# Two transformer blocks on one core: another order of splits, products and norm sums in nine stages, and x times the mixed rows' root in place of the reciprocal

## The reference

```python
# block one
h = rmsnorm(x, g_mix); z = h @ w_in                       # 1024 x 2560: b_gate, c_gate, x_in, u, v
y_conv = b_gate * conv3(c_gate * x_in)                    # 512 channels, 3 taps, causal
y_sgu  = gelu(u) * (tril(w_spatial) @ layernorm(gelu(v), g_sgu) + b_spatial)   # 8 heads, chunks of 128
x = x + concat(y_conv, y_sgu) @ w_out                     # 1024 x 1024
t = rmsnorm(x, g_ffn)
# router: top 1 of 4 groups, top 2 of its 8 experts; y = sum over 32 experts, each weighted per token
x = x + sum_e((silu(t @ w_gate[e]) * (t @ w_up[e]) * comb_e) @ w_down[e])       # d_expert 512
x = x + sigmoid(rmsnorm(x, g_ple) @ w_ple_gate) * (p @ w_ple_proj)              # p: 256 wide
x = rmsnorm(x, g_final)
# block two
h = rmsnorm(x, norm_mix_pre); proj = h @ w_in_2           # 1024 x 4608: conv_in, q, k, v, g_conv, g_att
u = silu(layernorm(conv31(glu(conv_in)), ...)); conv_out = u @ w_conv_branch + b
att_out = stick_breaking_attention(q, k, v) @ w_att_branch                      # 8 heads of 64
mix = (sigmoid(g_conv) * conv_out + sigmoid(g_att) * att_out) @ w_out_2
x = x + rmsnorm(mix, norm_mix_post)
gate, up = split(rmsnorm(x, norm_ffn_pre) @ w_ffn_up)     # 1024 x 5632
x = x + rmsnorm((silu(gate) * up) @ w_ffn_down, norm_ffn_post)                  # 2816 x 1024
```

## Time and profile before

| | |
|---|---|
| time before, median of 3 runs | 989.81 us (988.94 to 992.14) |
| the profiled execution's own time | 990.13 us |
| its span in the trace | 988.4 us |
| PE busy | 946.4 us (96%) |
| DVE busy | 497.4 us (50%) |
| ACT busy | 330.3 us (33%) |
| chain that ended last | PE 87%, DVE 7%, ACT 3%, issue 2%, DMA 1% |
| mean rate of the loads over the span | 293 GB/s |

### The profile page before, as it was taken

How to read it: one execution, slowest core, us unless ns; L and a number is a source line. 1 busy time by engine, 2 the same in 40 slices (tenths; PEclk the granted TensorE clock), 3 DMA queues, 4 the chain that set the end, 5 groups by cost and what they waited for, 6 DMA issues and landing times.

```text
span 988.4 us, 14242 instructions
## 1 busy us (share of the span) xinstructions
PE 946.4 (96%) x5926; PEld 670.2 (68%) x5926; DVE 497.4 (50%) x866; ACT 330.3 (33%) x527; POOL 36.1 (4%) x39
## 2 busy tenths in 40 slices
PE   6999999999999899999899899999999899999997
PEld 6997734444434444444344689978989899999885
DVE  6595612222222223222122776979898667676632
ACT  5823210101011010101001657555566555544531
POOL 1000000000000000000000000222310000000000
PEclk9999999999999999999999999999999999999999
DMA  8956999999999999999999942532433424555301
GB/s 324 406 233 260 424 407 427 420 430 432 429 430 431 426 431 430 431 430 431 431 425 419 432 189 115 212 129 96 161 133 124 170 107 180 189 201 200 128 1 42
DMA packets 28981, 289.45 MB, mean 293 GB/s; under 512 B 3056, under 2 KB 6384, under 8 KB 12400
## 3 DMA queue, kind: packets, MB, share of 16 engines
q1 hardware_dynamic: 28192, 286.91, 70.9%
q10 hardware_dynamic: 720, 1.57, 0.4%
HBM read 287.43 MB, written 1.05 MB: 292 GB/s over the span
## 4 chain that ended last, share of the span: by engine, by line
PE 87%; DVE 7%; ACT 3%; issue 2%; DMA 1%; SPq 0%; DVEq 0%; ACTq 0%
PE ps L282 86%; DVE wl L278 2%; DVE arena L1531 1%; ACT wh L271 1%; DMA arena<-in_xT 1%; PE ps L1045 1%; DVE arena L589 0%; ACT arena L1835 0%; DVE arena L1737 0%; ACT arena L1838 0%; DVE arena L378 0%; PE ps L2017 0%; ACT in_h L660 0%; DVE arena L1439 0%; DVE arena L584 0%
## 5 line engine op out<-in xcount | busy, mean ns | idle before, releaser
L282 PE MATMUL ps<-ring,arena 128*64 128x512 f32 x1216 | 340.1, 599 | 7.0 <-issue 6.7
L282 PEld LDWEIGHTS ps<-ring,arena 128*64 128x64 f32 x1216 | 109.7, 138 | 166.9 <-issue 164.6
L278 DVE TENSOR_TENSOR wl<-ring,wh 128x1024 fp32r<-128x1024 f32 x150 | 180.2, 1232 | 59.6 <-ACT wh L271 59.4
L271 ACT ACTIVATE wh<-ring 128x1024 fp32r<-128x1024 f32 x150 | 151.0, 1049 | 38.5 <-PE ps L282 28.2
L282 PE MATMUL ps<-arena 128*64 128x512 f32 (+3 forms) x416 | 161.4, 538 | 0.7 <-DVE arena L584 0.5
L1150 DVE SCALAR_TENSOR_TENSOR arena<-ps,arena 128x512 f32<-128x512 f32 x16 | 12.0, 750 | 205.7 <-PE ps L282 205.7
L282 PE MATMUL ps<-up_h,wh 128*128 128x256 f32 x352 | 87.0, 285 | 3.9 <-ACT up_h L1937 3.9
L282 PEld LDWEIGHTS ps<-arena 128*64 128x64 f32 (+1 forms) x416 | 53.2, 141 | 47.0 <-issue 41.2
L282 PE MATMUL ps<-up_l,wh 128*128 128x256 f32 x352 | 83.0, 283 | 0.0
L1220 ACT ACTIVATE y_h<-ps 128x512 fp32r<-128x512 f32 x32 | 19.1, 597 | 158.1 <-PE ps L282 158.1
L282 PEld LDWEIGHTS ps<-up_h,wh 128*128 128x128 f32 x352 | 67.1, 191 | 4.3 <-issue 4.3
(11 more groups left out here) (263 smaller groups left out, 1508.0 us busy)
## 6 DMA issues: line engine op xcount, KB each, us to landing
ring<-in_moe SPq DMA_DIRECT2D x69, 2048.0 KB, 24.2
arena<-in_moe SPq DMA_DIRECT2D x17, 2048.0 KB, 25.9
ring<-in_w_in SPq DMA_DIRECT2D x12, 2048.0 KB, 10.5
ring<-in_w_up SPq DMA_DIRECT2D x11, 2048.0 KB, 7.7
ring<-in_moe SPq DMA_DIRECT2D x20, 512.0 KB, 15.0
ring<-in_w_dn SPq DMA_DIRECT2D x5, 2048.0 KB, 7.7
ring<-in_w_out SPq DMA_DIRECT2D x4, 2048.0 KB, 15.9
arena<-in_moe SPq DMA_DIRECT2D x12, 512.0 KB, 13.1
```

The lines of the kernel that those rows point to most:

```text
L271: e.activation(wh(i), raw_piece(i), ACT.Copy).then_inc(*hi.up(i))
L278: e.tensor_tensor(wl(i), raw_piece(i), wh(i), SUB).then_inc(*lo.up(i))
L282: return e.matmul(o, l, r, start=first, stop=final, skip_group_check=True)
```

## The change

Line numbers in the diff are left out; names are as above.

1. Table of slots, w_ple_proj. It is loaded no longer as a tile of the stream, but into its own place PPW, behind the first expert tile d 0. The tables of slots move by one, so that the last tiles of the experts and the first of what follows lie in other slots.

```diff
-N0 = 8
+N0 = 7
-SLOTS = ([0, 1, 2, 3, 8, 0, 1, 2], [3, 8, 0, 1, 9, 5, 7, 4, 6, 2], [2, 3, 0, 1])
+SLOTS = ([0, 1, 2, 3, 8, 0, 1], [2, 3, 8, 0, 9, 1, 5, 7, 4, 6], [2, 3, 0, 1])
...
+                if (name, n) == ("d", 0):
+                    e.dma_start(PPW, dr["w_pp"][0].rearrange("p (c n) -> p c n", c=2)).then_inc(l_xk, 16)
```

```diff
-            for j in range(4):
+            def spatial(j):
...
             for j in range(4):
                 e.wait_ge(*cgate.at(j))
                 three(e, ps[CB[j]][:, 0:256], "in1", 4, j, XGH, XGL)
+                if j == 1:
+                    e.wait_ge(*msk.at(0))
+                    e.wait_ge(*vn.at(1))
+                    for x in range(4):
+                        spatial(x)
...
-                split_lo(e, j + 19)
+                split_lo(e, j + 20)
+            split_lo(e, 24)
...
+            gated(0)
+            gated(1)
+            rest(0)
+            rest(1)
...
+            gated(2)
+            for c in (4, 5, 6, 7, 2):
+                rest(c)
+            split_lo(e, 25)
+            gated(3)
+            split_lo(e, 26)
+            rest(3)
```

```diff
+                if q == NP - 1:
+                    split_hi(e, FIRST + 1)
...
-                    split_lo(e, FIRST + 1)
                     add(q, 0)
-            split_lo(e, FIRST + 2)
             add(NP - 1, 1)
```

```diff
-                e.tensor_scalar(XN[:, j, :], XT[:, j, :], vcol("g_final", j), None, M).then_inc(*xn.up(j))
...
-                e.scalar_tensor_tensor(out=H5L[:, j, :], in0=XN[:, j, :], scalar=vcol("pre2", j), in1=H5H[:, j, :],
+                e.scalar_tensor_tensor(out=H5L[:, j, :], in0=XT[:, j, :], scalar=gpre[:, j:j + 1], in1=H5H[:, j, :],
...
-                split_lo(e, FIRST + (8 if j < 4 else 10 if j == 4 else 12))
+                split_lo(e, FIRST + (8, 8, 9, 10, 12, 12, 12, 12)[j])
```

```diff
             for j in range(4):
+                if j == 3:
+                    softplus_dve(e, 0)
...
-            softplus_dve(e, 0)
...
-            recip(e, "r4", RB[:, 1, :])
-            e.wait_ge(*recips.at("r4"))
-            for c in range(8):
-                e.tensor_tensor(XT[:, c, :], XN[:, c, :], RB[:, 1, :], M).then_inc(*x4.up(c))
-                if c == 5:
-                    softplus_dve(e, 2)
+            taps_dve(e, 12)
+            softplus_dve(e, 2)
             taps_dve(e, 6)
...
-                taps_dve(e, 4)
+                taps_dve(e, 3)
```

```diff
+            e.wait_ge(*sum6.at("all"))
+            mm(e, ps[4][:, 0:256], inv1024, SQM[:, 0, :], True, False)
+            e.wait_ge(*sq6.at(7))
+            mm(e, ps[4][:, 0:256], inv1024, SQM[:, 7, :], False, True).then_inc(*means.up("r6"))
...
             split_lo(e, OUT2 + 14)
-            recip(e, "r6", R6)
-            e.wait_ge(*recips.at("r6"))
+            e.wait_ge(*roots.at("r6"))
             for j in range(9):
                 if j < 8:
-                    e.wait_ge(*mx.at(j))
-                    e.tensor_tensor(MX[:, j, :], MX[:, j, :], R6, M).then_inc(*mxr.up(j))
+                    e.wait_ge(*x4.at(j))
+                    e.tensor_tensor(XT[:, j, :], XT[:, j, :], R6, M).then_inc(*x4s.up(j))
```

```diff
-            mean(e, ps[7][:, 0:256], SQM, inv1024, [sq7.at(c) for c in range(8)], "r7")
...
+                    if (key, jj) == ("g", 2):
+                        e.wait_ge(*sum7.at("all"))
+                        mm(e, ps[7][:, 0:256], inv1024, SQM[:, 0, :], True, True).then_inc(*means.up("r7"))
```

```diff
+            for h in range(2):
+                b = ps[2 + h][:, :]
+                for k in range(16, 22):
...
-                e.wait_ge(*proj.at("fdn", 21, i))
                 for n in range(2):
+                    e.wait_ge(*(proj.at("fdn", "half") if (i, n) == (1, 0) else proj.at("fdn", 21, i)))
...
+                    e.tensor_tensor(OUT[:, i, sl], ps[2 * i + n][:, :], GB[:, sl], M).then_inc(*o_n.up(i, n))
                 recip(e, "o%d" % i, rr)
```

More of the change, by code:

```diff
@@ L50, in stream @@
 def stream():
-    out = [("in1", i) for i in range(5)] + [("out1", i) for i in range(2)] + [("pproj", 0)]
+    out = [("in1", i) for i in range(5)] + [("out1", i) for i in range(2)]
     out += moe_order()
@@ L176, in build @@
         WL = nc.alloc_sbuf_tensor_at("wl", [128, 8, 1024], R32, offset=ring_at + 24 * SLOT)
-        pieces = [(key, j) for key in order if key[0] not in ("g", "u", "d", "pproj") for j in range(2 if key == ("fdn", 5) else 4)]
+        pieces = [(key, j) for key in order if key[0] not in ("g", "u", "d") for j in range(2 if key == ("fdn", 5) else 4)]
         n_piece = {k: i for i, k in enumerate(pieces)}
@@ L409, in build @@
         wsv = WS[:, 0:4, :].rearrange("p a (h t) -> p (a h) t", h=2)
-        made = sig("made", ["eps", "ones", "zpad", "gsq"])
+        made = sig("made", ["eps", "ones", "zpad", "gsq", "gpre"])
         xg_h = sig("x_hi", range(8))
@@ L501, in part @@
                 e.wait_ge(*bgate.at(2 * n + i))
[L502 removed]
+                wide(e, ps[CB[2 * n + i]][:, :], "out1", n, i, MIXH, MIXL, mix, ((0, 1, 4, 5), (6, 7, 2, 3)))
             def turn(n):
@@ L691, in mixer_act @@
             root(e, "vv", VV, VV)
-            split_hi(e, 22)
-            for j in range(4):
-                e.wait_ge(*mixed.at(j))
-                e.activation(MIXH[:, 4 + j, :], Z[:, j, 2:258], ACT.Copy).then_inc(*mix_h.up(4 + j))
-            for j in range(4):
-                e.wait_ge(*bgate.at(j))
-                e.activation(MIXH[:, j, :], CR[:, j, :], ACT.Copy).then_inc(*mix_h.up(j))
-                split_hi(e, j + 23)
+            split_hi(e, 24)
+            for c in (0, 1, 4, 5, 6, 7, 2, 3):
+                if c < 4:
+                    e.wait_ge(*bgate.at(c))
+                    e.activation(MIXH[:, c, :], CR[:, c, :], ACT.Copy).then_inc(*mix_h.up(c))
+                else:
+                    e.wait_ge(*mixed.at(c - 4))
+                    e.activation(MIXH[:, c, :], Z[:, c - 4, 2:258], ACT.Copy).then_inc(*mix_h.up(c))
+                split_hi(e, {0: 25, 1: 26, 2: 27}.get(c, 0))
         def out1_act(e):
@@ L1636, in in2_act @@
             root(e, "r45", R45, ps[7][:, 0:256], squared=1)
+            for was in emptied(*last_in(8)):
+                e.wait_ge(*was)
             e.wait_ge(*means.at("r4"))
-            root(e, "r4", RB[:, 1, :], ps[6][:, 0:256])
+            root(e, "r4", R4, ps[6][:, 0:256])
             e.preload_act_table_set("sigmoid_and_others")
@@ L1895, in build @@
         sq6 = ca_sq.then(range(8))
+        sum6 = sig("sum6", ["four", "six", "pair", "all"])
+        sum7 = sig("sum7", ["eps", "four", "two", "one", "all"])
         mx = sig("mx", range(8))
-        mxr = sig("mxr", range(8))
+        x4s = sig("x4s", range(8))
+        s6 = sig("s6", ["turned", "column"])
         x5 = sig("x5", range(8))
@@ L1955, in out2_dve @@
                                            in1=XUH[:, j - 1, :], op0=M, op1=SUB).then_inc(*up.up(j - 1))
+            e.scalar_tensor_tensor(out=ES, in0=R6, scalar=8 * EPS, in1=R6, op0=M, op1=M).then_inc(*sum7.up("eps"))
+            e.wait_ge(*sq7.at(7))
+            e.tensor_tensor(SQM[:, 0:4, :], SQM[:, 0:4, :], SQM[:, 4:8, :], ADD).then_inc(*sum7.up("four"))
+            e.wait_ge(*sum7.at("four"))
+            e.tensor_tensor(SQM[:, 0:2, :], SQM[:, 0:2, :], SQM[:, 2:4, :], ADD).then_inc(*sum7.up("two"))
+            e.wait_ge(*sum7.at("two"))
+            e.tensor_tensor(SQM[:, 0, :], SQM[:, 0, :], SQM[:, 1, :], ADD).then_inc(*sum7.up("one"))
+            e.wait_ge(*sum7.at("one"))
+            e.tensor_tensor(SQM[:, 0, :], SQM[:, 0, :], ES, ADD).then_inc(*sum7.up("all"))
             split_lo(e, OUT2 + 16)
@@ L2087, in down_pe @@
                 part(k, 1)
-            for x in range(2):
+            for k in range(16, 22):
+                part(k, 0)
+            for h in range(2):
+                b = ps[2 + h][:, :]
                 for k in range(16, 22):
-                    part(k, x)
+                    i = n_piece[("fdn", k // 4), k % 4]
+                    for v in (WH, WL):
+                        r = v[:, i % 8, h * 512:h * 512 + 512]
+                        z = mm(e, b, FFH[:, k, 128:256], r, False, k == 21 and v is WL)
+                        if v is WH:
+                            mm(e, b, ffl(k)[:, 128:256], r, False, False)
+                    if h:
+                        z.then_inc(*proj.up("fdn", k, 1))
+                    elif k == 21:
+                        z.then_inc(*proj.up("fdn", "half"))
         def down_act(e):
```

150 lines of the change are left out of this document (82 added, 68 removed).

## The result

The changed kernel takes 966.71 us (median of 4 runs, 965.25 to 968.42) against 989.38 us (median of 4, 987.65 to 992.14): ratio 0.977, 95% interval 0.9749 to 0.9791. Its profiled execution took 968.42 us, span 966.7; a second one (run a_again) 968.57 us, span 966.8.

What follows compares the result with a forecast made beforehand. PE, busy 96% of the span, was taken as the bound, with loads setting the experts' end. Stage gains summed to 19.7 us, taken from the profiled 990.1 to give 970.5 us, range 967.0 to 977.0.

Steps and rivals of the forecast that it cites:

- In1 and out1: End of in1 and start of out1: PE's pauses of 0.80 and 1.02 go, 1.8 us gained, bounds 0 and 2.3.
- Expert stage: Experts: PE starts 1.8 us earlier, w_ple_proj's 1 MB no longer ahead of the loads gives 1.3; together 3.1.
- Experts to ple: Handover to ple: earlier last adds give 0.95 us, the low clock stretch going gives 1.5; together 2.45.
- Ple, in2, att: PE's waits go: 2.4 us before in2 (low split), 1.9 in in2 (softplus_dve), 1.3 in att (L1737).
- Out2: Out2 to fup: PE has the mean 2.6 us earlier, a reciprocal of 1.76 goes; together 4.35, bounds 3.0 and 4.6.
- Rival B: DVE becomes the bound of out2 and fup's start; out2 gives 1.8 instead of 4.35; 974 to 977 us; chance 0.15.
- Fup: Fup: eight products of 3.27 us become one of 0.43 and two transposes; 2.6 us gained, bounds 1.0 and 2.6.
- Tail: Behind PE's last product: one square instead of two, GB products beside root and sum; 1.6 us gained, bounds 0.6 and 1.9.
- A: Rival: loads absorb the experts' earlier start, 3.1 us lost; 973.6 us, 974 with the handover partly lost; chance 0.14.
- D: Rival: PE repeatedly starves for low pieces in fup, 3.8 us each; slower than before, 993 us; chance 0.03.
- E: Rival: moved slots make the tiles behind the experts late and eat the sum; 990 us; chance 0.02.
- C: Rival: the clock stands at 783 too and the loads give all the 2.4 us; 967.9 us; chance 0.09.

Runs made afterwards that it cites:

- a_again: The changed kernel run once more with nothing changed: 966.98 us, span 966.8.
- b_pp: The kernel before with only the table of slots and w_ple_proj's place changed: 989.97 against 989.84 us, ratio 0.9995.
- b_eight: The kernel before with one number changed, ACT splitting in1's pieces up to 8 instead of 9 after root r1: 988.36 against 991.4 us.
- a_nine: The changed kernel with ACT's split number put back to 9 instead of 8: 968.68 us, against 966.98 for the changed kernel.
- a_fill: The changed kernel with ten products of constants on PE in its pause between out2 and fup: 965.58 us, ratio 0.9752.
- a_soft: The changed kernel with softplus_dve 0 behind the last piece of K and its split, as before: 968.68 us.
- a_best: The changed kernel with ten products of constants in PE's pause before fup and four more DVE taps ahead of a split: 963.94 us, ratio 0.9727.
- a_tail: The changed kernel with the end of fdn and the tail as before: 969.24 us.
- a_hand: The changed kernel without ACT's early split in the last pair of experts: 968.36 us, ratio 0.9779.
- a_ones6: The changed kernel with the mixed rows' squares summed by eight PE products as before, without DVE's four additions: 968.70 us.
- a_ones7: The changed kernel with r7's mean by eight PE products as before, DVE's additions for it taken out: 970.53 us.
- a_ple: The changed kernel with DVE's two low splits back between the experts' last adds and ACT's first pgate split behind the experts: 967.82 us.
- b_mix: The kernel before with only the new order of in1 and out1 on PE, DVE and ACT: 986.15 against 989.84 us, ratio 0.9958.

## Why the prediction was off, by its steps

The sum started at 990.13, the profiled execution; the median before is 989.38, so 0.75 of the 3.8 between forecast and measured median is the starting point, more than the 0.3 by which the range was missed. (990.13 less 19.7 is 970.4, not 970.5.) The other 3.0 are gain that the sum does not have.

**In1 and out1, the step that failed.** The prediction's term for this stretch was 1.8, the two pauses 0.80 and 1.02, bounds 0 to 2.3. Up to out1 alone 3.8 and 5.0 were measured. The working counted the pauses that one profile shows and passed over a line of the diff, `split_hi(e, 9)` to 8, in the same functions. In the profile before, the wait that this line ends measured 0.17 us, because PE was late there by chance; b_pp shows it at 2.27, b_eight takes it away (out1 2.7 earlier), and a_nine puts it back (out1 3.9 later, 2.16 by the pause and the rest by the clock behind it). The late pauses are worth about 1.6 to 1.9, as forecast, though not by the pauses named: 0.54 and 0.80 went, 1.02 became 0.74. The order of the splits adds the other 2 to 3.5, a term that the sum put at nothing without a reason.

**Expert stage.** That the end follows PE's start was right: where out1 moved by 3.9 (a_nine), the last product moved by 4.2. The 1.3 for the 1 MB does not show; b_pp's profile has nothing of it, and its medians leave it open. From about 150 us on the loads run without a gap, and from there to the last expert tile they took 392.6 to 396.4 us over the profiles. The 0.2 and 1.7 of the ledger lie within this spread, and the 1.02 of the late pause, of which 0.28 went, lies in this line too.

**Experts to ple.** 0.95 was 0.4. The pause at ple_h fell by 1.4, but the one ahead of it grew from 0.61 to 1.55, since ACT's early split is a new wait. The 1.5 for the clock was right in this profile: 0.53 became 1.00. Behind a pause of 2.2 to 2.3 before ple the clock fell in six of seven profiles, behind 0.9 in none of ten. The Trainium skill, TensorE: Matmul & The Clock Gate, "Part 1: The HAM clock gate", has idleness halve the clock and activity restore it; the rows agree, and a_fill and the two kernels like it agree most directly, since nothing but PE's activity was changed at that place.

**Ple, in2, att.** 3.9 and 3.2 against 4.3 / 3.9 and 3.4 / 3.1. Ple was right. In in2 and att the size came out in part by luck. The 1.9 of softplus_dve stands (a_soft: 1.8 to 2.1). But the 1.3 at L1737 was used up by a new pause of 1.4 at the last tap, which a_best then removed: PE's pauses over the two stages went from 3.56 us to 1.90, 1.7 less. The other 1.5 to 1.7 lie in no pause; at least part of it is that the same products follow each other faster (220 starts in in2 take 27.47 us before and 27.20 in both profiles of the changed kernel).

**Out2.** 4.35 was 3.8 / 3.9; the reciprocal gave 1.9 for 1.76, the products 1.6 for 2.6. DVE's additions end 0.5 to 0.9 us behind PE, which the count of DVE's list (780.6 against 779.9) had said and I had set to even. Rival B was right in kind and small in size. The eight products moved here take 0.47 to 0.48 us each in the changed kernel, against 0.616 where they stood.

**Fup.** 2.6 was 2.5 / 3.1. The products give 3.0; the longer low clock takes 1.2 of it in the first profile and nothing in the second; a faster pace of the products gives 0.9 and 0.2 back, and fdn takes 0.3 more, for which no run has the cause. So the 2.5 came near the forecast by luck. That the clock could also get worse was not in the range. No late split showed.

**Tail.** 1.6 was 1.9: the 0.5 set aside for the second GB product was too much; L2186 runs to 962.45 and the reciprocal starts at 962.58. From the end of PE's last product to the end of DVE's work it takes 3.0 us instead of 4.9 (3.3 was the sign named); the store behind it is not in these numbers.

Rivals A, D and E did not happen. C's number, 967.9, is the nearest, for another reason than it gave.

## What to carry to other kernels

A wait of 0.2 us in one profile can be the rest of a wait of 2 us that does not show because the waiting engine happened to be late itself; so look for what an engine in order is stuck on (ACT 4.45 us at a load), not only for who waits for it. When the diff renumbers a count in such an engine's program, ask for each what stands behind it. And where PE pauses for 2 us in front of matmul work, products without use in the pause can keep its clock up, as here at 768 us.

## What the runs showed of the chip

- The half clock level around the same pause of 2.1 us before fup lasted about 6.8 us in the first profile of the changed kernel and in a_tail, about 3.4 us in its second profile and in a_soft, a_hand, a_nine, a_ones6 and a_ones7, and was absent in a_ple, with the same instructions around it.
- Behind the pause of 2.4 us before in2 (kernel before, b_pp, b_mix, b_eight) the clock fell in one of four profiles, b_eight, where it takes 60.8 us instead of 59.0 from the start of in2 to its first 128x512 product.
- Within fup the same 24 products take 2.70, 2.73 or 2.76 us (first to last start) at a granted clock of 1.00, and the pace changes within one execution, in several profiles behind one of the two groups of transposes. Over the last 38 pieces of fup this makes up to 1.3 us between two profiles. In in2 it is 2.73 or more in the four profiles with the old order there and 2.70 in eleven of the thirteen with the new one. What sets it stays open.
- Medians moved less than profiles in a_fill (1.1 against 2.7) and a_nine (1.7 against 3.5). The runs of one kernel spread by 1.2 to 6.4 us within a comparison, and the profiled execution was the slowest of its kernel's runs in nine of sixteen, both times for the changed kernel, and the fastest in two (a_fill, a_ple). So stretches of a profile say where, and only medians over runs how much.
